# Two mixers of a transformer kernel: norms and operand tiles taken into the head loops

## The reference

```python
# gated linear attention: 4 heads of 256 value columns
o = gla_chunked(qh, kh, vh, la_f, False) + flip(gla_chunked(flip(qh), ..., True))
o = rms_norm(o, g_out).reshape(bsz, seq, GLA_DV)     # over the 256 columns of a head
return (o * jax.nn.silu(r)) @ w_out                  # 1024 x 1024

# differential attention: 8 heads of 128 value columns, two softmaxes each
a = pr[:, :, 0] - lam * pr[:, :, 1]
o = einsum('bhqk,bhkd->bhqd', a, vt)
o = rms_norm(o, g_sub) * (1.0 - lambda_init)         # over the 128 columns of a head
return o.reshape(bsz, seq, D_MODEL) @ w_out          # 1024 x 1024
```

## Time and profile before

| what | value |
|---|---|
| median of 3 runs | 1129.81 us (1126.03 to 1134.69) |
| the profiled execution | 1127.35 us, span 1125.6 us |
| granted TensorE clock, mean | 0.984 |
| TensorE busy | 1064.8 us (95%) |
| VectorE busy | 720.5 us (64%) |
| ScalarE busy | 554.3 us (49%) |
| POOL busy | 223.8 us (20%) |
| read from HBM | 190.83 MB, 170 GB/s over the span |

### The profile page before, as it was taken

One profiled execution on the slowest core, in us unless ns is written; L12 is line 12 of the kernel. 1 busy time (PEld: TensorE's weight loads), 2 busy tenths in 40 slices (PEclk: granted clock), 3 DMA queues, 4 the chain that ended last, 5 costly groups with the idle time before them and its releaser, 6 DMA issues.

```text
span 1125.6 us, 20288 instructions
## 1 busy us (share of the span) xinstructions
PE 1064.8 (95%) x7913; PEld 984.5 (87%) x7913; DVE 720.5 (64%) x1127; ACT 554.3 (49%) x954; POOL 223.8 (20%) x248
## 2 busy tenths in 40 slices
PE   5999988999999899989999999979987999999998
PEld 5577677999999698879999999978865899999998
DVE  4785777777645567748565645666768766564554
ACT  2223555544454666327454544655446764544453
POOL 0110002323312121012333311141110133332102
PEclk9999989999999999999999999989998999999999
DMA  9962464577557354404555456644440264645651
GB/s 351 400 266 75 150 237 138 168 248 265 153 157 223 103 205 142 159 1 143 191 191 180 147 155 191 225 150 150 150 150 1 76 225 160 212 133 148 202 191 39
DMA packets 183556, 192.78 MB, mean 171 GB/s; under 512 B 5881, under 2 KB 143394, under 8 KB 183490
## 3 DMA queue, kind: packets, MB, share of 16 engines
q1 hardware_dynamic: 182480, 191.15, 50.3%
q0 software_dynamic: 144, 0.52, 0.2%
q10 hardware_dynamic: 866, 0.21, 0.1%
HBM read 190.83 MB, written 1.05 MB: 170 GB/s over the span
## 4 chain that ended last, share of the span: by engine, by line
PE 56%; DVE 5%; ACT 2%; issue 2%; POOL 1%; POOLq 0%; ACTq 0%
PE gemm L1978 17%; PE gemm L1980 17%; PE gemm L1979 17%; PE aux L2438 1%; DVE wlo L1321 1%; PE aux L2100 1%; PE aux L2502 1%; ACT whi L867 1%; DVE state L1873 1%; PE aux L2496 1%; DVE neg_max L1937 1%; DVE d_p L1953 0%; DVE g_b L1827 0%; PE gemm L2528 0%; ACT ohi L1103 0%
## 5 line engine op out<-in xcount | busy, mean ns | idle before, releaser
L1321 DVE TENSOR_TENSOR wlo<-raw,whi 128x1024 fp32r<-128x1024 f32 (+2 forms) x324 | 369.1, 1184 | 78.7 <-ACT whi L867 78.2
L1978 PE MATMUL gemm<-ohi,whi 128*128 128x256 f32 x1376 | 388.7, 283 | 1.7 <-DVE wlo L1321 1.4
L1979 PE MATMUL gemm<-olo,whi 128*128 128x256 f32 x1376 | 385.6, 280 | 0.0
L1980 PE MATMUL gemm<-ohi,wlo 128*128 128x256 f32 x1376 | 384.5, 279 | 0.0
L867 ACT ACTIVATE whi<-raw 128x1024 fp32r<-128x1024 f32 (+2 forms) x324 | 288.7, 956 | 66.0 <-PE gemm L1980 50.9
L1978 PEld LDWEIGHTS gemm<-ohi,whi 128*128 128x128 f32 x1376 | 259.7, 189 | 5.1 <-issue 2.6
L1979 PEld LDWEIGHTS gemm<-olo,whi 128*128 128x128 f32 x1376 | 259.9, 189 | 0.6 <-issue 0.5
L1980 PEld LDWEIGHTS gemm<-ohi,wlo 128*128 128x128 f32 x1376 | 259.7, 189 | 0.0
L1980 PE MATMUL gemm<-acthi,wlo 128*128 128x256 f32 x528 | 147.8, 280 | 0.0
L1978 PE MATMUL gemm<-acthi,whi 128*128 128x256 f32 x528 | 147.5, 279 | 0.0
L1979 PE MATMUL gemm<-actlo,whi 128*128 128x256 f32 x528 | 147.3, 279 | 0.0
(11 more groups left out here) (351 smaller groups left out, 1509.5 us busy)
## 6 DMA issues: line engine op xcount, KB each, us to landing
raw<-in_ffn_w_in SPq DMA_DIRECT2D x44, 1024.0 KB, 6.2
raw<-in_ffn_w_out SPq DMA_DIRECT2D x32, 704.0 KB, 5.8
part<-in_w_ada SPq DMA_DIRECT2D x32, 512.0 KB, 10.5
raw<-in_gla_w_in SPq DMA_DIRECT2D x6, 2048.0 KB, 7.6
raw<-in_diff_w_in SPq DMA_DIRECT2D x6, 2048.0 KB, 7.6
raw<-in_w_gate SPq DMA_DIRECT2D x11, 1024.0 KB, 6.4
raw<-in_w_up SPq DMA_DIRECT2D x11, 1024.0 KB, 8.6
raw<-in_w_down SPq DMA_DIRECT2D x16, 704.0 KB, 5.4
```

The lines of the kernel that those rows point to most:

```text
L1321: dve.tensor_tensor(wlo[hslot][:, q * w:(q + 1) * w], raw[slot][:, q * w:(q + 1) * w], whi[hslot][:, q * w:(q + 1) * w].bitcast(F32), ALU. ...
L1978: pe.matmul(dst, st_hi, mv_hi, start=start, stop=False)
L1979: pe.matmul(dst, st_hi, mv_lo, start=False, stop=False)
L1980: return pe.matmul(dst, st_lo, mv_hi, start=False, stop=stop_)
```

## The change

In gated linear attention the squares of heads 0 and 1 are summed inside the last `outputs` call, into `X[3]`; all outputs now go through `X[2]`. Their root and their four tiles are made before the last read-out, into buffers of their own (`gom`, `ghi`, `glo`), because the old places still hold live data. Head 2's squares are summed behind the last outputs, and head 3's inside the out projection, behind its k = 1 (`beside`). Roots and tiles of heads 2 and 3 follow one head at a time. In differential attention the transposes all use `X[0]`; the squares of pairs 0 and 1 (heads 0 to 3) and their sums are taken inside the loop, pair 0's root too, and pair 0's two tiles are made in the last two rounds. Pair 2 is summed behind the last values, pair 3 inside the out projection behind its k = 1; roots and tiles come pair by pair. Both `keep_warm` calls ahead of the out projections are gone.

```diff
--- before
+++ after
@@ -353,6 +353,7 @@
+ghi, glo, gom = sb("ghi", 4 * T, F32R, at=U + 9216), sb("glo", 4 * T, F32R, at=W + 512), sb("gom", 4 * T, at=W + 512)
@@ -468,6 +469,12 @@
+def gla_operand(early, late):
+    return lambda t: tl(early, t) if t < 4 else tl(late, t)
+gated_om, gated_hi, gated_lo = gla_operand(gom, om), gla_operand(ghi, xhi), gla_operand(glo, xlo)
+pick = lambda b, t: b(t) if callable(b) else tl(b, t)
@@ -1215,18 +1222,33 @@
-    for h in range(GH + 1):
+    def gated_square(h):
+        act.wait_ge(go_read, h + 1)
+        me.did(act.activation(tl(g_sq, 2 * h, 2), tl(g_o, 2 * h, 2), ACT.Square), sq_ready)
+    for h in range(GH):
...
-        else:
-            act.wait_ge(go_read, h)
-            me.did(act.activation(tl(g_sq, 2 * h - 2, 2), tl(g_o, 2 * h - 2, 2), ACT.Square), sq_ready)
-    roots([(G[n], g_rs[:, 512 * n:512 * n + 512]) for n in range(2)], 1.0 / GDV, 1)
-    prep(hi=xhi, free=PH["gla_r"].tile0 + 8)
+        elif h < GH:
+            gated_square(h - 1)
+    def gated_high(*tiles):
+        for t in tiles:
+            me.next(om_ready)
+            me.did(act.activation(gated_hi(t), gated_om(t), ACT.Copy), ohi_ready)
+    roots([(X[3], g_rs[:, 0:512])], 1.0 / GDV, 1)
+    gated_high(0, 1, 2, 3)
+    gated_square(GH - 1)
+    root(X[1], T, 1.0 / GDV, 1, g_rs[:, 512:768])
+    gated_high(4, 5)
+    root(X[0], T, 1.0 / GDV, 1, g_rs[:, 768:1024])
+    gated_high(6, 7)
@@ -1274,6 +1296,15 @@
+    def pair_root(g, bank):
+        roots([(bank, tl(d_nsq, 2 * g, 2))], 1.0 / (2 * HD), 1)
+    def high_parts_of(*tiles):
+        for t in tiles:
+            me.next(om_ready)
+            me.did(act.activation(tl(xhi, t), tl(om, t), ACT.Copy), ohi_ready)
@@ -1287,16 +1318,25 @@
-        if i == NH:
-            squares((0, 1), d_o, d_nsq)
+        if i in (5, 7):
+            squares((i // 2 - 2,), d_o, d_nsq)
...
-            me.did(act.activation(tl(d_pt, (i - 1) % 2, w=512), X[(i - 1) % 2][:, :], ACT.Copy), pt_ready)
-    squares((2, 3), d_o, d_nsq)
-    roots([(G[g], tl(d_nsq, 2 * g, 2)) for g in range(4)], 1.0 / (2 * HD), 1)
-    prep(hi=xhi, free=PH["diff_v"].tile0 + 4)
+            me.did(act.activation(tl(d_pt, (i - 1) % 2, w=512), X[0][:, :], ACT.Copy), pt_ready)
+        if i == 6:
+            pair_root(0, X[1])
+    wait(act, tile_done, PH["diff_v"].tile0 + 4)
+    high_parts_of(0, 1)
+    squares((2,), d_o, d_nsq)
+    pair_root(1, X[1])
+    high_parts_of(2, 3)
+    squares((3,), d_o, d_nsq)
+    pair_root(2, X[0])
+    high_parts_of(4, 5)
+    pair_root(3, X[1])
+    high_parts_of(6, 7)
@@ -1853,7 +1893,7 @@
-        me.did(dve.tensor_copy(tl(g_o, 2 * h, 2), X[2 + h % 2][:, :]), go_read)
+        me.did(dve.tensor_copy(tl(g_o, 2 * h, 2), X[2][:, :]), go_read)
@@ -1877,17 +1917,29 @@
+    def make(*tiles):
+        for t in tiles:
+            if t in (0, 4, 6):
+                me.next(sd_ready)
+            if t % 2 == 0:
+                me.next(gated)
+            me.did(dve.scalar_tensor_tensor(gated_om(t), tl(g_r, t), B("gla_g_out_2", t % 2), tl(g_rs, t // 2),
+                                            ALU.mult, ALU.mult), om_ready)
+    def gated_low(*tiles):
+        for t in tiles:
+            me.next(ohi_ready)
+            me.did(dve.tensor_tensor(gated_lo(t), gated_om(t), gated_hi(t).bitcast(F32), ALU.subtract), olo_ready)
+    make(0, 1, 2, 3)
+    gated_low(0, 1)
...
-    def make(t):
-        if t % 4 == 0:
-            me.next(sd_ready)
-        if t % 2 == 0:
-            me.next(gated)
-        return dve.scalar_tensor_tensor(tl(om, t), tl(g_r, t), B("gla_g_out_2", t % 2), tl(g_rs, t // 2),
-                                        ALU.mult, ALU.mult)
-    prep(make, free=PH["gla_r"].tile0 + 8, hi=xhi, lo=xlo)
+    gated_low(2, 3)
+    make(4, 5)
+    gated_low(4, 5)
+    make(6, 7)
+    gated_low(6, 7)
@@ -1929,6 +1981,17 @@
+    make_tile = group_make(d_o, d_nsq, lambda t: lam[:, 5:6])
+    def make_pair(g):
+        for t in (2 * g, 2 * g + 1):
+            me.did(make_tile(t), om_ready)
+    def low_pair(g):
+        for t in (2 * g, 2 * g + 1):
+            me.next(ohi_ready)
+            me.did(low_part(t, tl(om, t), xhi, xlo), olo_ready)
@@ -1954,11 +2017,17 @@
+        if i == NH + 1:
+            wait(dve, tile_done, PH["diff_v"].tile0 + 4)
+            make_pair(0)
+        if i == NH + 2:
+            low_pair(0)
...
-    me.again(mixed_ready)
-    prep(group_make(d_o, d_nsq, lambda t: lam[:, 5:6]), free=PH["diff_v"].tile0 + 4, hi=xhi, lo=xlo)
+    for g in range(1, 4):
+        make_pair(g)
+        low_pair(g)
@@ -1986,7 +2055,7 @@
-             operand=(ohi, olo), wide=6):
+             operand=(ohi, olo), wide=6, beside=None):
@@ -2015,11 +2084,13 @@
-                                    *[tl(b, k) for b in operand], n_ == 0, n_ == KT - 1)
+                                    *[pick(b, k) for b in operand], n_ == 0, n_ == KT - 1)
+                    if beside and n_ in beside:
+                        beside[n_]()
...
-                                    *[tl(b, order[n_]) for b in operand], False, n_ == KT - 1)
+                                    *[pick(b, order[n_]) for b in operand], False, n_ == KT - 1)
@@ -2056,7 +2127,7 @@
-                        mv = [tl(b, k + 2 * layer) for b in src]
+                        mv = [pick(b, k + 2 * layer) for b in src]
@@ -2417,9 +2488,19 @@
+    def head_squares(h, bank, c0, last):
+        if c0 == 0:
+            banks.claim(bank, sd_ready)
+        me.next(sq_ready)
+        for e in range(2):
+            ins = pe.matmul(bank[:, c0:c0 + T], ones[:, :], tl(g_sq, 2 * h + e), start=(e == 0), stop=(e == 1))
+        if last:
+            ins.then_inc(stat_done, 1)
...
-        bank = X[2 + h % 2]
+        bank = X[2]
@@ -2430,6 +2511,9 @@
+        if h == GH - 1:
+            head_squares(0, X[3], 0, False)
+            head_squares(1, X[3], T, True)
@@ -2474,18 +2558,10 @@
-    for h in range(GH):
-        if h % 2 == 0:
-            banks.claim(G[h // 2], sd_ready)
-        me.next(sq_ready)
-        for e in range(2):
-            ins = pe.matmul(G[h // 2][:, (h % 2) * T:(h % 2 + 1) * T], ones[:, :], tl(g_sq, 2 * h + e),
-                            start=(e == 0), stop=(e == 1))
-        if h % 2:
-            ins.then_inc(stat_done, 1)
+    head_squares(2, X[1], 0, True)
...
-    keep_warm(X[2], 2)
-    gemm("out1", dve_read, olo_from=start, operand=(xhi, xlo))
+    gemm("out1", dve_read, olo_from=start, operand=(gated_hi, gated_lo),
+         beside={1: lambda: head_squares(3, X[0], 0, True)})
@@ -2538,15 +2614,15 @@
-            banks.claim(X[s], pt_ready)
+            banks.claim(X[0], pt_ready)
...
-                    ins = pe.transpose(X[s][:, kt * T + qt * P:kt * T + (qt + 1) * P],
+                    ins = pe.transpose(X[0][:, kt * T + qt * P:kt * T + (qt + 1) * P],
...
-        if i == NH + 1:
-            group_stats((0, 1), ones[:, :], d_nsq, G[0:2])
+        if i in (6, 8):
+            group_stats((i // 2 - 3,), ones[:, :], d_nsq, X[1:2])
@@ -2555,10 +2631,10 @@
-    group_stats((2, 3), ones[:, :], d_nsq, G[2:4])
+    group_stats((2,), ones[:, :], d_nsq, X[0:1])
...
-    keep_warm(X[2], 4)
-    gemm("out2", dve_read, olo_from=start, operand=(xhi, xlo))
+    gemm("out2", dve_read, olo_from=start, operand=(xhi, xlo),
+         beside={1: lambda: group_stats((3,), ones[:, :], d_nsq, X[1:2])})
```

## The result

The changed kernel takes 1119.52 us (median of 5 runs, 1117.48 to 1122.71) against 1131.47 (5 runs of the kernel before, 1126.03 to 1134.69): a ratio of 0.9917, 95% interval 0.9891 to 0.9943. The two medians themselves lie 12 us apart (1.06%); where this text gives a gain from many runs, it goes by the ratio. The profiled execution took 1117.48 us, its span is 10.0 us shorter than before. The first fence is the page of the changed kernel, span and busy times, against the earlier trace rows: TensorE is as full as before, with 8 us less work under way, most of it the warming matmuls.

The account below looks back on a forecast made before the run. TensorE's instruction stream, busy 1064.8 of 1125.6 us, was taken to bound the kernel. Gains of 4.7 us (gated linear attention) and 3.0 us (differential attention), with warming removal at nothing, sum to 7.7: 1129.81 to 1122 us, range 1115 to 1129.

Parts of the forecast that it names:

- Place one, 4.7 us: Gated linear attention: `out1` starts 5.7 us earlier, head 3's squares cost 0.9 inside it; 4.7 us taken as gain.
- Place two, 3.0 us: Differential attention: `out2` starts 5.6 us earlier, but the second slab's low parts limit the gain to 3.0 us.
- The term for pair 0's root: Differential attention score loop: the root delays head 7's exponentials, adding 1.2 us to the path.
- the start of `out2`: Differential attention: `out2` starts at 873.3, 5.6 us before 878.90.
- ScalarE's road to the second slab: Differential attention: high parts, squares and roots in turn let the second slab's copies start at 881.2, 2.0 us earlier.
- The new wait: Second slab of `out2`: TensorE waits 1.4 us for low parts.
- the 0.3 us for later evictions: Differential attention: 0.3 us off the gain because evictions run later against TensorE.
- Warming matmuls, priced at nothing: Ahead of both out projections: removal costs nothing, since remaining holes of at most about 1.4 us keep the clock.
- rival B: Both places: no wait at `out2`'s second slab, head 7's exponentials not held up; gain 10.7 us, time 1119; chance 0.12.
- A: Second slabs: ScalarE and VectorE set their start; gain 2.5 us, time 1127.3, or 5, time 1125; chance 0.18.
- C: Start of an out projection: clock falls, one slab 9 us longer; 1131, or 1140 at both places; chance 0.04.
- D: Out projections: nothing gained, operand tiles come late and `out1` stops at k = 4; chance counted with the second-slab rival's.

Follow-up runs that it names:

- place_one: Only the gated linear attention half of the change, made to the kernel before: 1123.33 us (10 runs), ratio 0.9941 to the kernel before.
- act_delay: Changed kernel plus one unread 128 x 1024 ScalarE copy at each place, ahead of the second slab's copies: 1119.1 us (one execution).
- fill_hole: Kernel before plus 4 warming instructions in the 1.72 us hole of the gated linear attention loop's last round: 1128.47 us (12 runs), ratio 0.9972.
- root_later: Changed kernel with pair 0's root one head later, behind head 7's exponentials: 1120.47 us (6 runs), ratio 0.9907 to the kernel before.
- warm_back: Changed kernel with the warming matmuls put back ahead of each out projection, in a bank nobody waits for: 1125.47 us (one execution).
- nowarm_before: Kernel before with only the two groups of warming matmuls ahead of the out projections taken out: 1134.19 us (10 runs), ratio 1.0028.
- place_two: Only the differential attention half of the change, made to the kernel before: 1126.92 us (10 runs), ratio 0.9968 to the kernel before.
- both: Changed kernel with pair 0's root one head later and 6 warming instructions in the score loop's first hole: 1118.71 us (6 runs), ratio 0.9881.
- early_quarter: Changed kernel, pair 0's root later, score loop's first hole filled, one second-slab quarter ahead of the last two operand tiles: 1117.98 us (6 runs), ratio 0.9886.

## Why the prediction was right, and where it was off

The mechanism and the range held: 1122 forecast, 1119.5 measured. A gain of 7.7 us was forecast; the ratio of 0.9917 says 9.4 us (6.4 to 12.3), a move of 0.8% and so within 1%, though the two medians lie 1.06% apart. By its own steps:

**Place one, 4.7 us.** Right to a tenth: 4.79 in the profile, 4.74 in place_one. The first sums hid behind the state steps (the 24 matmuls start 0.06 us behind the states, as before), the read-out slipped as described (my 500.5 against 499.44 is 499.69 against 498.93 with everything 0.51 us earlier: 0.8, not 1.1), and the second slab met TensorE with a stop of 0.2 us. act_delay shows that both sides were indeed level there. What I missed is that the end of the second slab's readiness isn't the last low part but the eviction of tile 0 behind it on VectorE, 0.4 us later. That the sum came out to a tenth is partly luck: the last low part itself was there 0.3 us sooner than I had it (511.51 + 0.51 = 512.02 against 512.35), and the two errors cancel.

**Place two, 3.0 us: mis-sized.** The profile has 4.6. Of this 0.7 us isn't the change: the loop of before ran partly at a clock of 0.54 in its profile and took 29.89 us, where place_one's, the same code at 1.00, took 29.21. So 3.9 at equal clocks, as a sum of pieces: 29.21 + 10.60 + 22.69 - 58.59. No single profile shows the old code undisturbed. In place_one the clock fell just behind the stretch that I took from it, and its stage d is 11.53 us and not 10.60; fill_hole has a fall in the loop and another in stage d (11.27). The windows of place_one there:

```profile
860.00:864.00 4.00, 3.14 (x13) 2.41 (x14) 3.19 (x10) 2.54 (x7) 0.00 (x0) 0.69 0.00 0
864.00:868.00 4.00, 4.00 (x14) 2.71 (x13) 0.43 (x1) 1.11 (x2) 0.00 (x0) 0.89 0.00 0
```

So against these two the changed kernel's c + d + e is 4.8 us shorter.

The term for pair 0's root was right (1.2 forecast, 1.1 by root_later), and so was the start of `out2`: 3.5 us behind the last transposes. Off was ScalarE's road to the second slab. I had its copies start 11.85 us behind the last probability tiles; they start 10.84 behind (874.27 - 863.43). I had charged 0.6 us and more for each instruction of a long run, its full duration, where the next one can start before that is over:

```profile
865.35 0.62 ACT L938 ACTIVATE d_nsq<-d_o 128x512 f32<-128x512 f32 x1
865.87 0.68 ACT L929 ACTIVATE d_nsq<-aux,eps 128x512 f32<-128x512 f32 x1
866.58 0.63 ACT L932 ACTIVATE d_nsq<-d_nsq 128x512 f32<-128x512 f32 x1
```

The square shows 0.62 us, and 0.10 of it lies under the logarithm behind it; the exponential, which reads the logarithm's result, starts 0.03 us behind its end. Seven overlaps of 0.1 us between 864.24 and 874.27 make 0.7 of the 1.0 us; the rest isn't broken down. The Trainium skill (ScalarE: Activation LUTs, section "What ACT_TABLE_LOAD costs") says that back-to-back activations overlap by about 93 ns; this trace agrees where the second doesn't read the first one's result, with that 0.10. The new wait came, of 0.65 us rather than 1.4, released by an eviction and not by `wlo` as I had written, and the 0.3 us for later evictions is part of it and not to be added.

**Warming matmuls, priced at nothing.** Right for the changed kernel: its clock is 1.00 wherever they stood, and warm_back says they would now cost 1.8 and 3.2 us. But my reason was half right. I held that only a hole like the 2.78 us in the score loop costs the clock. The clock falls also at the hole of 1.72 us in the last round of the head loop, in two of the three profiles that have it, and I had this hole in hand (`[1.72 <-DVE state L1873]`) as free cover for the new sums and didn't ask what it does to the clock. The Trainium skill (TensorE: Matmul & The Clock Gate, section "HAM oscillation — how this bites in real kernels") describes a clock that falls at waits between bursts and must be won back each time; two profiles here agree with it, with 0.52 and 0.50 behind the hole, while a third, that of before, kept 1.00 behind the same hole.

**What this adds to the sum.** 4.8 + 3.9 = 8.7 us at equal clocks; the ratio says 9.4, and its interval (6.4 to 12.3) holds 8.7 too, so nothing more has to be explained. fill_hole alone gives a ratio of 0.9972, 3.2 us (0.9 to 5.4), as a fall that costs 3.3 us would if it happened in a good part of the executions. If that is the cause, the changed kernel gains by it as well, and my rival B named it ("the slow stretch [...] may also fall otherwise") but set it in the score loop and as noise of either sign. A rival stands beside it: the clock also falls in the score loop or just behind it in all four profiles of the old code there (before, place_one, nowarm_before, fill_hole) and in three of the five of the new code that leave the loop's first hole (place_two, act_delay, warm_back; not changed and root_later). How the medians' gain divides between these isn't shown.

**Rivals.** A (given back at the second slab) is the right mechanism with a small price: 0.2 and 0.65 us of stops. C happened only in nowarm_before, for 1.5 us. D did not happen: no wait at k = 4 or 6.

**Open.** How often the fall at the last round happens in the kernel before wasn't counted: two of three profiles have it, and the mean clocks give only the estimate above; why one execution has it and the next hasn't isn't settled. That the version both (or early_quarter) is faster than the changed kernel is shown in the stages (1.0 and 2.0 us) and not by the medians.

## What to carry to other kernels

A serial tail of squares, roots and tiles between a head loop and a projection can be taken in pieces: what belongs to finished heads goes into the holes of the loop, and the projection starts on the first tiles while the last are being made. What it is then worth can be read at the next thing the same helper engines must have ready, here the second weight slab and the eviction behind it. And a hole in TensorE's stream can cost more than its length (1.72 us idle, 3.3 us more behind it): look at the granted clock behind each hole in more than one profile, and put the moved work into those holes first.

## What the runs showed of the hardware that I had not expected

The granted clock fell behind a hole of 1.72 us in two profiles (0.52 at 500 us in place_two; 0.76 and then 0.50 in nowarm_before) and not in that of before, with the same instructions. Behind 3.03 us of idle time in nowarm_before `out1` started at 1.00, and behind 4.15 us `out2` at 0.60. So the length of one hole alone doesn't tell whether the clock falls. The price was some 3.3 us at the last round, 1.5 us at the start of `out2` and 0.2 to 1.3 us in the score loop (place_two 30.53 against 30.33, nowarm_before 30.51 against 29.21).
